# Where the second layer's expert table is split into float16 halves: 47 of its 128 chunks earlier, through DRAM, and no subtraction on GpSimd

## The reference, cut to what matters

```
q = (ht @ wq).reshape(n_tok, PEER_HEADS, PEER_QDIM)
s1 = einsum('thd,kd->thk', q[..., :PEER_HALF], k1); s2 = einsum('thd,kd->thk', q[..., PEER_HALF:], k2)
t1, i1 = lax.top_k(s1, 16); t2, i2 = lax.top_k(s2, 16)        # then the 16 best sums of pairs, softmax g
def block(hb, ib, gb):                                          # ib: the chosen experts of each token
    ue, ve = jnp.take(u, ib, axis=0), jnp.take(v, ib, axis=0)
    act = jax.nn.gelu(jnp.einsum('td,thkd->thk', hb, ue), approximate=False)
    return jnp.einsum('thk,thkd->td', gb * act, ve)
```

## Time and profile before

| what | us |
|---|---|
| median of 3 runs (4318.37 to 4331.03) | 4329.03 |
| the profiled execution, its own time | 4331.53 |
| its span, first to last instruction | 4329.8 |
| second layer: norm, 2867 to 2966 | 99 |
| second layer: scores, 2966 to 3071 | 105 |
| second layer: choice and activation, 3071 to about 3720 | 649 |

### The profile page before, as it was taken

The page is one execution under the profiler, slowest core; times in us unless marked ns, Lnnn a source line. Parts: engine busy times, 40 slices in busy tenths (PEclk is TensorE's granted clock), DMA queues, the critical chain, the costliest instruction groups (busy, mean ns, idle before and its releaser), DMA issues. The chain is left out here.

```text
span 4329.8 us, 59390 instructions
## 1 busy us (share of the span) xinstructions
PE 3731.4 (86%) x19545; PEld 1931.0 (45%) x19545; DVE 3186.7 (74%) x6186; ACT 1332.3 (31%) x1722; POOL 1663.6 (38%) x1191
## 2 busy tenths in 40 slices
PE   6888779789988898599999978877989888699996
PEld 1555565454434343344444424434545455344442
DVE  2547654539878788689999976843689788588887
ACT  0326521221212121222333305831334334333331
POOL 0400000230323232367887811203344344277774
PEclk8999989899999999899999989988999999899998
DMA  4946754596999998899999962212588797799995
GB/s 205 345 163 221 233 155 152 194 317 212 324 356 322 346 350 333 312 364 403 404 404 404 404 235 72 74 64 84 188 291 304 273 345 244 290 344 341 347 343 219
DMA packets 416426, 1188.55 MB, mean 275 GB/s; under 512 B 40112, under 2 KB 126960, under 8 KB 409584
## 3 DMA queue, kind: packets, MB, share of 16 engines
q1 hardware_dynamic: 240956, 639.75, 41.2%
q0 software_dynamic: 110592, 402.70, 25.7%
q10 hardware_dynamic: 64708, 143.91, 8.6%
...
## 5 line engine op out<-in xcount | busy, mean ns | idle before, releaser
L2097 PE MATMUL ex_R<-ex_vl,hh 128*128 128x512 f16 x1792 | 683.0, 381 | 0.0
L1665 PE MATMUL ca_A<-hh,ca_us 128*128 128x512 f16 x2048 | 634.3, 386 | 50.5 <-ACT ca_ga L1706 39.3
L2097 PE MATMUL ex_R<-hl,hh 128*128 128x512 f16 x1792 | 543.5, 382 | 93.8 <-DVE hh L2111 72.3
L1633 POOL DMA_INDIRECT ca_ug<-in_peer_u_rows,chosen_rows x288 | 293.9, 1020 | 660.6 <-DVE ca_ug L1790 538.7
L2128 DVE SCALAR_TENSOR_TENSOR ex_sum<-ex_vg,ex_share,ex_sum 128x1024 f32<-128x1024 f32 x384 | 493.4, 1285 | 9.8 <-DVE ex_share L2120 6.0
L2025 POOL DMA_INDIRECT ex_vg<-in_peer_v_rows,ex_index x384 | 388.5, 1012 | 190.3 <-issue 85.0
L1706 ACT ACTIVATE ca_ga<-ca_A 128x512 f32<-128x512 f32 (+1 forms) x256 | 139.4, 544 | 897.1 <-PE ca_A L1665 710.9
L1665 PE MATMUL ca_A<-hh,ca_uh 128*128 128x384 f16 x1024 | 345.5, 337 | 77.2 <-DVE ca_ul L1760 32.5
L1790 DVE SCALAR_TENSOR_TENSOR ca_ug<-ca_ug,ca_hp 128x1024 f32<-128x1024 f32 x288 | 346.7, 1216 | 84.4 <-DMA ca_ug<-in_peer_u_rows,chosen_rows 82.5
L1665 PE MATMUL ca_A<-hl,ca_us 128*128 128x512 f16 x1024 | 394.8, 386 | 0.0
L2136 DVE TENSOR_TENSOR ACC<-ACC,ex_R 128x512 f32<-128x512 f32 x448 | 305.8, 683 | 92.5 <-PE ex_R L2097 89.5
(11 more groups left out here) (384 smaller groups left out, 7126.4 us busy)
## 6 DMA issues: line engine op xcount, KB each, us to landing
ex_vr<-in_peer_v SPq DMA_DIRECT2D x256, 512.0 KB, 9.1
ca_us<-u_parts SPq DMA_DIRECT2D x128, 512.0 KB, 6.4
ca_ur<-in_peer_u SPq DMA_DIRECT2D x128, 512.0 KB, 5.2
...
acts<-ca_ga ACTq DMA_DIRECT2D x128, 256.0 KB, 6.1
...
ex_ar<-acts SPq DMA_DIRECT2D x128, 256.0 KB, 11.9
acts<-ca_ga ACTq DMA_DIRECT2D x128, 192.0 KB, 4.0
```

Of the source, the lines that this page charges most:

```text
L1633: nc.gpsimd.indirect_dma_start(ug[x % UG][:, :], None, u_rows, bass.IndirectOffsetOnAxis(ap=chosen_rows[:, x:x + 1], axis=0)).then_inc(ug_ ...
L1665: last = nc.tensor.matmul(A[b][:, a:a + w], lhs[:, k, :], rhs[:, k, a:a + w], start=(k == 0 and x == 0), stop=(k == KD - 1 and x == 2))
L2097: last = nc.tensor.matmul(R[(NP * q + y) % BANKS][:, :], lhs[q][:, x, o:o + P], rhs[q][:, x, h * 512:h * 512 + 512], start=(x == 0 and n = ...
```

## The change

- `READY[1]` names 47 chunks of the second layer: x of 4 and more with x mod 8 in (0, 4, 6). They are split ahead: 27 in the norm `n1` (`SPLIT_NORM1`, 5, 5, 5, 5, 3, 2, 2 in the seven passes of the loop) and 20 in the scores (`SPLIT_SCORES1`), and stored to a new tensor `u_parts1`. In the norm SP waits for the last store before the stage ends.
- In `choose_and_activate` a ready chunk is loaded as two halves straight into the ring, once TensorE is done with chunk x - 4; the 81 others are loaded raw. SP's list is in the order of the chunks.
- ScalarE casts only the raw ones (77 besides the first four, before 124), VectorE makes all their low halves (77, before 62), GpSimd none (before 62). GpSimd's list holds gathers only.

```diff
+READY = (range(PCH), [x for x in range(4, PCH) if x % 8 in (0, 4, 6)])
+SPLIT_NORM1 = (5, 5, 5, 5, 3, 2, 2)
+SPLIT_SCORES1 = (1, 1, 2) * 5
@@ project_and_norm, SyncE
-                        rows.move(sp, 0, SPLIT_NORM, SPLIT_NORM)
-                        rows.all_stored(sp, SPLIT_NORM)
+                        rows.move(sp, 0, sum(split), sum(split))
+                        rows.all_stored(sp, sum(split))
@@ project_and_norm, VectorE, at the end of pass i
-                        if rows is not None and 1 <= i < SPLIT_NORM + 1:
-                            rows.low(dve, i - 1)
+                        behind = 1 if tag == "n0" else 0
+                        for x in range(sum(split[:max(0, i - behind)]), sum(split[:i + 1 - behind])) if rows is not None else ():
+                            rows.low(dve, x)
-LOW_BY = (None, ("gpsimd", "vector", "gpsimd", "vector"))
@@ peer_scores, SyncE
                     for x in range(N):
-                        if rows is not None and len(groups[x]):
+                        if len(groups[x]):
                             rows.move(sp, groups[x].start, groups[x].stop, upto[-1])
                         if x + 3 < N:
                             weights(x + 3)
...
+                    for j in range(0 if layer == 0 else RING):
                         sp.dma_start(ring.ur[j][:, :, :], io["peer_u"][layer][j].rearrange("p (k n) -> p k n", k=KD)).then_inc(ring.u_in[j], 16)
+                    rows.all_stored(sp, upto[-1])
@@ choose_and_activate, SyncE
-                    with sp.Fori(2, PCH // RING) as k:
-                        for j in range(RING):
-                            sp.wait_ge(u_cut[j], k * cut[j] - cut[j])
-                            sp.dma_start(ur[j][:, :, :], u_src[bass.ds(k * RING + j, 1)].rearrange("o p (k n) -> p (o k) n", k=KD)).then_inc(u_in[j], 16)
+                    for x in range(RING, PCH):
+                        j = x % RING
+                        if x in ring.number:
+                            sp.wait_ge(first_done, x + 1)
+                            sp.dma_start(us[j][:, :, :, :].rearrange("p x k n -> p (x k n)"), parts[ring.number[x]].rearrange("p x n -> p (x n)")).then_inc(u_cut[j], 16)
+                            continue
...
+                            sp.wait_ge(u_cut[j], ring.cut_upto[x - RING])
+                        sp.dma_start(ur[j][:, :, :], u_src[x].rearrange("p (k n) -> p k n", k=KD)).then_inc(u_in[j], 16)
@@ choose_and_activate, GpSimd
-                    for x in range(0 if ready else PCH):
-                        if x >= RING:
-                            low(x // RING, x % RING)
-                        while issued < SLOTS and (pre if issued < UG else chunk_of_dot(issued - UG)) + 2 <= x:
-                            gather(issued)
-                            issued += 1
@@ choose_and_activate, VectorE
-                        if not ready and low_by[j] == "vector" and not (isinstance(n, int) and n * CT + x < RING):
+                        if not ready and n * CT + x >= RING and n * CT + x not in ring.number:
```

More of the change, by code:

```diff
@@ L221, with __init__ @@
 class TableSplit:
-    def __init__(self, nc, io, parts, first, raw, cut, raw_in, high_made, low_made, stored):
-        self.nc, self.table, self.parts, self.first, self.raw, self.cut = nc, io["peer_u"][0], parts, first, raw, cut
+    def __init__(self, nc, io, parts, layer, first, raw, cut, raw_in, high_made, low_made, stored):
+        self.nc, self.table, self.parts, self.first, self.raw, self.cut = nc, io["peer_u"][layer], parts, first, raw, cut
+        self.chunks = READY[layer]
         self.raw_in, self.high_made, self.low_made, self.stored = raw_in, high_made, low_made, stored
@@ L233, in load @@
             sp.wait_ge(self.low_made, i - len(self.raw) + 1)
-        sp.dma_start(self.raw[r], self.table[self.first + i]).then_inc(self.raw_in[r], 16)
+        sp.dma_start(self.raw[r], self.table[self.chunks[self.first + i]]).then_inc(self.raw_in[r], 16)
     def store(self, sp, i):
@@ L264, in table_split @@
 @contextmanager
-def table_split(nc, io, parts, first, tag, raw=(), cut=()):
+def table_split(nc, io, parts, first, tag, raw=(), cut=(), layer=0):
     with ExitStack() as c:
@@ L1092, in project_and_norm @@
                 mw_in0, mw_in1, mw_in2, mbias_in, mprod, madded, mstored, *w_in):
-            rows = c.enter_context(table_split(nc, io, parts, SPLIT_FIRST[4], tag, early["raw"], early["cut"])) if parts is not None else None
+            split = {"n0": (1,) * SPLIT_NORM, "n1": SPLIT_NORM1}.get(tag, ())
+            first_split = {"n0": SPLIT_FIRST[4], "n1": SPLIT_FIRST1[0]}.get(tag)
+            rows = c.enter_context(table_split(nc, io, parts, first_split, tag, early.get("raw", ()), early.get("cut", ()), layer)) if parts is not None else None
             mw_in = (mw_in0, mw_in1, mw_in2)
@@ L1181, in _ @@
                             high(i - 3)
-                        if rows is not None and i < SPLIT_NORM:
-                            rows.high(act, i)
+                        for x in range(sum(split[:i]), sum(split[:i + 1])) if rows is not None else ():
+                            rows.high(act, x)
                 @block.vector
@@ L1739, in _ @@
                     nc.scalar.activation(hp[:, :], HS[:, :], ACT.Copy).then_inc(rows_ready, 1)
-                    schedule(act, chunk, load_scores, exponentials, lambda n: None, gate_step, store)
+                    schedule(act, chunk, load_scores, exponentials, lambda n: None, gate_step, store, unrolled=not ready)
                     for b in range(2):
```

98 lines of the change are left out of this document (38 added, 60 removed).

## The result

The changed kernel took 4362.78 us (median of 4 runs, 4357.95 to 4368.16) against 4328.59 of the kernel before (4 runs): a ratio of 1.0083, 95% interval 1.0067 to 1.0100. That is slower, inside the forecast range, 7 us above its value. The profiled execution has a span of 4365.0 us, 35.2 more than before.

A forecast was written before the change was run, and what follows sets the result against it. PE sets the pace in scores and gate stretches; where experts are chosen it waits, at most 45.2 us the change's to take. 26 + 0.6 + 12 + 12 - 24 = +27, so 4356 us; range 4338 to 4378, 8 in 10 4320 to 4385.

The forecast's parts named there:

- Norm, +26: Second layer's norm: splitting 27 chunks there makes the stage end 26 us later, bounds +16 and +32.
- The third group: Norm: the third group of five chunks ends at about 2940.5, so the last gather begins 2 us late.
- Scores, loop, +12: Second layer's scores: PE waits 3.9, 2.0, 3.9, 2.0 us for matrices after products with two chunks, +12 together.
- the failed step: Scores loop: with two chunks beside product x, matrix x + 3 is ready 16.1 us after the product ends.
- my upper bound: Scores loop: +20 us if single chunks stall too and the clock falls after each wait.
- Scores, tail, +12: From product 14 to the choice: 23 us where it was 10.9, `ca_ur` loads now behind the last chunks; bounds +6, +16.
- Choice, -24: Second layer's choice and activation: -6.6 us at the first crossing, -8.6 at the second and third; sum -24.
- my bound of -48: Choice: the largest gain, if all 45.2 us of PE's low-half waits go and a little clock comes back.
- Rival A: Choice: the lock rules everything, all 45.2 us go and clock returns, -67 against +51, 4313 us; chance 0.12.
- 4.7 us to the end of the low half: Second crossing: VectorE needs 4.7 us from its cast's start to the low half's end, where it needed 6.7.
- B: Norm and scores: the early splitting hides, costs 27 us against a gain of 24, 4332, no change; chance 0.17.
- C: Choice: raw loads behind ready chunks on SP hold ScalarE, then PE, 25 to 40 us; 4380 to 4395; chance 0.09.

The follow-up runs named there:

- e5_head_only: Changed kernel with 30 chunks ahead, not 47, none in the norm's tail; matrix loads ahead of stores, `ca_ur` loads beside product 12: 4274.11 us, 0.9879 of before.
- e9_crossings: Changed kernel with only nine chunks ahead, chosen around the crossings, three in each of the norm's first three passes, none in the scores: 4282.55 us.
- e3_weights_first: Changed kernel with SyncE issuing the load of matrix x + 3 ahead of product x's chunk stores and raw loads in the second layer's scores: 4331.46 us.
- e8_copies_between: Changed kernel with VectorE copying a pair's scores ahead of the low halves of the pair's second product, second layer: 4360.13 us.
- e1_vector_lows: Kernel before with VectorE making all 124 low halves of the second layer, GpSimd none, nothing split ahead: 4305.55 us.
- e7_idle_subs: e1_vector_lows with 62 GpSimd subtractions added in the second layer's choice, whose results nobody waits for: 4379.92 us.

## Why the prediction was right, and where it was not

**Bounds of the stages.** Right: the norm and the scores were the price, the choice the gain, and the gate stretches did shorten little (from chunk 33 to chunk 51 it took 89.3 before and 87.5 after; 4.8 us less in the three stretches together). PE's short waits for low halves inside them, 6.0 us before and 0.2 after, are what I had cancelled against raw loads that wait on SyncE.

**Norm, +26 for +30.5.** Of the 4.5, 4.0 were there before the tail began. The third group ended at 2942.5, in a stage that started 2.05 earlier, so 4.0 behind the forecast's 2940.5; its five chunks took 11.9 us, the far end of the 10 to 12, its fourth waiting 4.08 for its cast. From there to the end of the last low half (2987.1) it was 44.6 us with 43.8 forecast, and 3.1 more to the next stage's load with 3.5. The misjudged part is the third group of five: it began the last gather 5.9 us late (2942.38, below, in a stage 2.05 earlier, for 2938.57), where I had 2. That the tail is paid and smaller first groups are not is shown by e5_head_only and e9_crossings (5, 5, 3 and 3, 3, 3 chunks in the first three passes: 94.9 and 94.7).

```profile
2930.53 3.49 DVE L262 TENSOR_TENSOR n_cut<-n_raw,n_cut 128x1024 f16<-128x1024 f32 x3
2938.11 1.23 DVE L262 TENSOR_TENSOR n_cut<-n_raw,n_cut 128x1024 f16<-128x1024 f32 x1 [4.08 <-ACT n_cut L257]
2941.24 1.22 DVE L262 TENSOR_TENSOR n_cut<-n_raw,n_cut 128x1024 f16<-128x1024 f32 x1 [1.91 <-ACT n_cut L257]
2942.38 1.22 DVE L1208 TENSOR_TENSOR n_y<-n_ps,n_vec 128x1024 f32<-128x1024 f32 x1
```

**Scores, loop, +12 for +32.9: the failed step.** It says that the matrix is ready 16.1 us after the product. Follow product 8, two chunks beside it, in the changed kernel (ScalarE, VectorE, SyncE, GpSimd, one view each):

```profile
3067.11 0.60 ACT L1406 ACTIVATE sc_qT<-sc_Q 128x512 f32<-128x512 f32 x1 [12.94 <-PE sc_Q L1384]
```

```profile
3068.69 4.51 DVE L262 TENSOR_TENSOR sc_cut<-sc_raw,sc_cut 128x1024 f16<-128x1024 f32 x2 [10.46 <-ACT sc_cut L257]
```

```profile
3074.07 0.76 SPq L1342 DMA_DIRECT2D sc_w<-in_peer_wq  x1
```

```profile
3083.25 1.89 POOL L1370 TENSOR_TENSOR sc_wh<-sc_w,sc_zero 128x1024 f16<-128x1024 f32 x1 [11.14 <-DMA sc_w<-in_peer_wq]
3085.22 2.12 POOL L1371 TENSOR_TENSOR sc_wl<-sc_w,sc_wh 128x1024 f16<-128x1024 f32 x1
```

The matrix is there at 3087.3, 20.2 us after the product's copy, not 16.1. The same steps in the first layer, in the kernel before, from which I had taken the 12.3 us from product to GpSimd (the copy at 929.22 and GpSimd's start at 941.48 are in the earlier trace rows):

```profile
931.01 2.36 DVE L261 TENSOR_TENSOR sc_cut<-sc_raw,sc_cut 128x1024 f16<-128x1024 f32 x2 [6.38 <-ACT sc_cut L256]
```

```profile
932.19 2.94 POOL L1362 TENSOR_TENSOR sc_wh<-sc_w,sc_zero 128x1024 f16<-128x1024 f32 x1 [3.15 <-DMA sc_w<-in_peer_wq]
```

```profile
934.48 1.33 SPq L1332 DMA_DIRECT2D sc_w<-in_peer_wq  x1
```

Two things make the 4.1. Here both low halves are blocked by GpSimd's split of another matrix, 4.51 us for 2.36; there GpSimd begins behind the first of them and it is GpSimd that is held, 2.94 us for 1.90. I had spoken of this blocking for the choice only, and not carried it to the scores, where the earlier trace rows show GpSimd busy for 56 of 104 us. And the load took 9.2 us from issue to use, where it was 7.0 there. From 3070.16 to 3075.97 SyncE issued eight transfers of 512 KB (three stores, three raw loads, two matrices). Why this load was slower is not shown: the stretch moved no more than the first layer's, and over the whole scores the median landing of `sc_w` is 6.2 us here, 7.0 in the first layer (and 3.2 in the second layer before). The windows are 3070.2 to 3083.3 in the changed kernel and 929.2 to 941.5 in the kernel before:

```profile
3070.20:3083.30 13.10, 9.08 (x50) 5.00 (x48) 6.64 (x5) 3.08 (x4) 1.96 (x2) 0.93 0.91 294
```

```profile
929.20:941.50 12.30, 12.30 (x81) 8.25 (x82) 4.89 (x5) 5.40 (x6) 5.08 (x3) 1.00 0.93 329
```

Product 8 is the worst of four. After the copies of products 2, 5, 8 and 11 the matrix was ready 17.5, 18.6, 20.2 and 19.0 us later. Behind product 2 the low halves were not blocked and ended 3.9 us after the copy; behind the other three they ended at 6.1 to 6.3. From issue to use the loads took 8.4, 6.4, 9.2 and 7.2 us. So the blocking makes three of the rounds late and a slow load two. When the matrix is due was forecast rightly: 12.2 us after product 8 and 14.0 after 5 and 11; only product 5 was due later than forecast, 14.0 after product 2 for 12.2, since product 3 had waited. That is why the longest wait, 8.2 us, is product 11's.

e3_weights_first leaves both low halves as blocked as they were and puts the matrix ahead in the queue, and 29.6 us go; e8_copies_between gives the third candidate 3 us. How the lateness divides between blocking and loads was not tried apart by a run. So in these four rounds PE waited 21.6 us where 11.8 were forecast, and 1.7 more at product 3. The second part of the miss is the slow products behind such waits, 8.8 us, for which the sum had nothing and only my upper bound something (+20, itself too low).

**Scores, tail, +12 for +12.1.** Right to the step: the last cast of `ca_ur` began at 3134.93, 13.1 behind the copy of product 14 (15 forecast for its end), the four subtractions ended at 3140.2 (18.3; 19.5), the first chunk at 23.0.

```profile
3134.93 0.69 DVE L1439 CAST ca_us<-ca_ur 128x1024 f16<-128x1024 f32 x1 [0.55 <-DMA ca_ur<-in_peer_u]
3135.54 4.62 DVE L1442 TENSOR_TENSOR ca_us<-ca_ur,ca_us 128x1024 f16<-128x1024 f32 x4
3140.08 1.28 DVE L1427 COPY sc_so<-sc_S 128x512 f32<-128x512 f32 x2
```

**Choice, -24 for -38.8.** The places were right and each was taken too small: up to the three crossings it gave -10.1, -15.2 and -11.7 for -6.6, -8.6 and -8.6, and -1.8 behind them. No operation of the f16 groups is above 0.694 us now, as forecast. Two things were too small. The clock had no term: the 7.6 us less of busy PE stand only in my bound of -48, as the slow products of the loop stood only in its bound. And the price of a GpSimd subtraction: the prediction took 1.8 us for blocked work in the first stretch, 4.0 at its crossing and 2.15 at the second, while over the choice 60.6 us of VectorE's time go with the 62 subtractions (e1_vector_lows), 1 us each, spread over one-hot tiles, low halves and the f32 operations of the choice. The Trainium skill says in "SBUF — State Buffer", "SBUF: two separate sides", that the two engines exclude each other on the shared port pair; e7_idle_subs agrees, +77.9 us for subtractions that nobody reads. My use of that rule was too narrow, in the choice and in the scores alike. Rival A had the mechanism and needed 64 us of gain; it got 38.8, since PE's waits for gelus (28.0 and 25.7) and those at the crossings stayed.

**The 4.84 at each crossing** I had counted as needed ("4.7 us to the end of the low half"). e9_crossings shows that they were the best place for a chunk ahead.

**Rivals.** B needed the norm and the scores to hide the work; none of the stages did. C, raw loads behind ready chunks, is seen but what passes on is small: ScalarE waits 95.8 us, 39 times, for `ca_ur` (before 5.2, 4 times), and PE's waits for low halves and gelus still fall.

```profile
ACT ca_us L1680 <- DMA ca_ur<-in_peer_u: 95.8, 39, 8.2
```
